# Three quarters of a down projection moved from one long matmul stage into the state loops of the following heads

## The chip, the cores and the metric

The kernel runs on one core of one Trainium2 chip. Its time is the device time of one launch, in microseconds (us); lower is better. The core has a matrix engine (TensorE, PE in the profile; its weight loads are PEld), a vector engine (VectorE, DVE), a scalar engine (ScalarE, ACT), GpSimd (POOL), and SyncE (SP), which here issues nearly all transfers. Sixteen DMA engines move data between memory and the on-chip buffer. Matmul results land in eight accumulation banks of 128 x 512 floats (`psum`).

## The reference

Two decoder layers run over 320 tokens at once: a prompt of 256 and eight sample sequences of 8. The change concerns layer 1, an mLSTM block with four heads; per head a sequence carries a state matrix C of 1024 x 1024 floats.

```
xm, z = split(xn @ w_up)                        # 4096 inner columns = 4 heads x 1024
q, k, v = blockdiag projections of conv(xm), xm
per head and sample sequence:
    num  = wprev * (q @ C) + (scores @ v);  h = num / max(|den|, exp(-m))
    C    = wC * C + (k * wS)^T @ v               # written out for every sequence
hn  = head_layernorm(h, norm_g)                 # per head
out = (hn + skip * xc) * silu(z)
y   = out @ w_down                              # 4096 x 2048
x   = x + y
```

After it come a mixture-of-experts layer (`moe`) and the last norm. All is float32.

## The kernel before

Activations lie transposed: 128 channels on the partitions, 320 tokens along the free side. `xm` holds the 32 chunks of inner channels (8 for each head), `m.x` the residual in 16 chunks of 128 output channels.

`mlstm` goes through heads 0 to 3. For each head there are three blocks of preparation (projections, scores, transposes), in which the layer norm of the head before it is also finished (`HeadNorm`, with `z` and the skip), and then a block with the **state loop**: eight sample sequences, and per sequence eight chunks c of 128 rows of C (512 KB each). For one chunk PE multiplies the queries with it (L2124), forms the outer product of keys and values in two halves (L2135, banks 5 and 6), and DVE scales the chunk and adds the halves (L2197). SP then stores the chunk (L2070) and loads a later one (L2065). The chunks live in eight slots; a slot is loaded again for the next sequence three chunks after its store was issued (`LAG`), and only once that store has landed. PE, DVE and SP each keep to the order written in the code and wait on semaphores. At chunks 1 and 2 PE also computes a piece of the prompt's new C (L2140), which ACT copies out (L2185) and SP stores in two halves at chunk 4 (L2081); at chunk 4 PE turns the keys and values of the next sequence (`turn`, L2114). The numerators of sequences 0 to 3 gather in bank 0 and those of 4 to 7 in bank 7; after the loop they are copied out by ACT and DVE (L2187, L2200).

After head 3's own layer norm, `linear` computes the whole of `out @ w_down`: 16 output tiles, each of 32 matmuls (L344) over all 32 inner chunks. With 32 chunks the eight weight slots of 1 MB make one column block of four tiles (`cbs` = 1), so there are four passes, and a pass can start only when DVE has added the four tiles of the one before (L398). One matmul in float32 is one matmul in the program and two instructions in the trace.

The lines at issue: `linear` L287 to L351 and L398; the state loop L2062 to L2207; the call L2237.

Of the kernel before, what the change touches and what calls it, by code (L numbers as in the profile page):

```python
# [13 lines left out]
ALU = mybir.AluOpType  # L14
# [6 lines left out]
P = 128  # L21
D = 2048
T_P = 256
B = 8
T_S = 8
T = T_P + B * T_S
# [6 lines left out]
H = 4  # L33
# [7 lines left out]
IC = DI // P  # L41
# [61 lines left out]
@contextmanager  # L103
def signal(m, name):

    yield m.signals.take()
    m.signals.held -= 1
# [170 lines left out]
def linear(nc, m, weights, kc, rhs, copy_to=None, conv=None, norm=None, fill=None):  # L278
# [6 lines left out]


    kg = kc // KPS  # L287
    cbs = NSLOT // kg
    width = TPB * P
    passes = weights.shape[1] // width // cbs  # L290
    w = weights.rearrange("(g k p) n -> p g k n", k=KPS, p=P)
# [1 line left out]
    with ExitStack() as ctx:  # L293
        def signals(name, n):
            return [ctx.enter_context(signal(m, f"{name}{i}")) for i in range(n)]

        landed = signals("landed", NSLOT)
        used = signals("used", NSLOT)
        tile_done = signals("tile_done", cbs)
        by_act = signals("by_act", cbs)  # L300
        by_dve = signals("by_dve", cbs)
# [4 lines left out]
        @block.sync  # L306
        def _(sp):
            def load(i, s):
                col = (i * cbs + s // kg) * width
                sp.dma_start(slots[:, s, :, :], w[:, s % kg, :, bass.ds(col, width)]).then_inc(landed[s], 16)  # L310

            for s in range(NSLOT):
                load(0, s)
            with sp.Fori(1, passes) as i:
                for s in range(NSLOT):
                    if s % kg < kg - 1:
                        sp.wait_ge(used[s], i)
                    else:
                        sp.wait_ge(tile_done[s // kg], i * TPB)
                    load(i, s)  # L320
            if fill is not None:
                for p in range(PAIRS):
                    sp.dma_start(fill[p * P:(p + 1) * P, :],
                                 m.x[:, :, :].rearrange("p c t -> p (c t)")[:, 0:D]).then_inc(filled, 16)
                sp.wait_ge(filled, 16 * PAIRS)

        @block.tensor
        def _(pe):
            if norm:
                norm.tensor(pe)  # L330
            with pe.Fori(0, passes) as i:
                for s in range(NSLOT):
                    cb, g = s // kg, s % kg
                    pe.wait_ge(landed[s], i * 16 + 16)
                    if g == 0:
                        if copy_to is not None:
                            pe.wait_ge(by_act[cb], i * TPB + TPB)
                        else:
                            pe.wait_ge(by_dve[cb], i * TPB + TPB)
                    for k in range(KPS):  # L340
                        if norm:
                            pe.wait_ge(norm.normed, g * KPS + k + 1)
                        for t in range(TPB):
                            mm = pe.matmul(m.psum[:, cb * TPB + t, 0:T], slots[:, s, k, t * P:(t + 1) * P],  # L344
                                           rhs(g * KPS + k), start=(g == 0 and k == 0),
                                           stop=(g == kg - 1 and k == KPS - 1))
                            if g == kg - 1 and k == KPS - 1:
                                mm.then_inc(tile_done[cb], 1)
                    if g < kg - 1:
                        mm.then_inc(used[s], 1)  # L350
# [1407 lines left out]
def mlstm(nc, m, I, O):  # L1758
# [35 lines left out]
    gates_and_z(nc, m, I, O, conv, xm, xc, wq, wk, wv, blk, bg, bgf, u_col, m0, wc_row, ml, wcol, n0)  # L1794

    c_slot = view(m.ring, 8192, HC, DH)
    s_t = [view(m.ring, 7424, T_P), view(m.ring, 7424 + T_P, P), view(m.ring, 7424 + T_P + P, 64)]
    vt = view(m.xn, 0, 3, DH)
    kt = view(m.xn, 3 * DH, 2, DH)
# [15 lines left out]
    for h in range(H):  # L1815
# [136 lines left out]

        states = ExitStack()
        landed = [states.enter_context(signal(m, f"state_landed{c}")) for c in range(HC)]
        c_in = I["state_mlstm_C"][0].rearrange("b h (c p) e -> b h c p e", p=P)
        LAG = 3
        with signal(m, "turned") as turned, signal(m, "copied") as copied, signal(m, "prompt_num") as prompt_num, \
                nc.Block() as block:
            @block.sync
            def _(sp):  # L1960
                for c in range(HC - LAG):
                    sp.dma_start(c_slot[:, c, :], c_in[0, h, c]).then_inc(landed[c], 16)

            @block.tensor
            def _(pe):
# [72 lines left out]
        with states as ctx:  # L2038
# [9 lines left out]
            num_kept = ctx.enter_context(signal(m, "num_kept"))  # L2048
            keys = ctx.enter_context(signal(m, "keys"))
            c_done = ctx.enter_context(signal(m, "c_done"))  # L2050
            c_kept = ctx.enter_context(signal(m, "c_kept"))
            c_stored = [ctx.enter_context(signal(m, f"c_stored{e}")) for e in range(2)]
            block = ctx.enter_context(nc.Block())
# [8 lines left out]
            @block.sync  # L2062
            def _(sp):
                def load(b, c):
                    sp.dma_start(c_slot[:, c, :], one(c_in, b)[h, c]).then_inc(landed[c], 16)  # L2065

                def sequence(b, more):
                    for c in range(HC):
                        sp.wait_ge(updated, b * (2 * HC) + (2 * c + 4))
                        sp.dma_start(one(c_out, b)[h, c], c_slot[:, c, :]).then_inc(stored[c], 16)  # L2070
                        if c < LAG:
                            if not (isinstance(b, int) and b == 0):
                                sp.wait_ge(stored[c - LAG + HC], b * 16)
                            load(b, c - LAG + HC)
                        elif more:
                            sp.wait_ge(stored[c - LAG], b * 16 + 16)
                            load(b + 1, c - LAG)
                        if c == HC // 2:
                            for e in range(2):
                                sp.wait_ge(c_kept, b * 2 + (e + 1))  # L2080
                                sp.dma_start(one(c_prompt, b)[:, e * 512:(e + 1) * 512],  # L2081
                                             c_stage[e]).then_inc(c_stored[e], 16)

                sequence(0, True)
                with sp.Fori(1, B - 1) as b:
                    sequence(b, True)
                sequence(B - 1, False)
                for c in range(HC):
                    sp.wait_ge(stored[c], 16 * B)
                for e in range(2):  # L2090
                    sp.wait_ge(c_stored[e], 16 + 16 * B)
# [18 lines left out]
            def _(pe):  # L2110
                def turn(i, odd):
                    for j, rep in enumerate((krep, vrep)):
# [3 lines left out]
                                           start=True, stop=True)  # L2116
                        mm.then_inc(turned, 1)

                def sequence(half, i, odd, last=False):
                    pe.wait_ge(queries, at(i, odd, 1, 1))  # L2120
                    for c in range(HC):
                        pe.wait_ge(landed[c], at(i, odd, 16, 16))
                        for j in range(4):
                            mm = pe.matmul(m.psum[32 * j:32 * j + 32, 7 * half, 0:256], q_one[odd][:, c, :],  # L2124
                                           c_slot[:, c, j * 256:(j + 1) * 256], start=False,
                                           stop=last and c == HC - 1, skip_group_check=True)
                        if c == HC - 1:
# [9 lines left out]
                        if c in (1, 2):  # L2137
                            pe.wait_ge(keys, at(i, odd, 1, 1))
                            for a in range(2):
                                mm = pe.matmul(m.psum[:, c, :], k_one[odd][:, a, :],  # L2140
                                               vt[:, a, (c - 1) * 512:c * 512], start=(a == 0), stop=(a == 1))
                            mm.then_inc(c_done, 1)
                        if c == HC // 2 and not last:
                            pe.wait_ge(c_kept, at(i, odd, 2, 2))
                            turn(i if odd == 0 else i + 1, 1 - odd)

                for half in range(2):
                    for j in range(4):
                        mm = pe.matmul(m.psum[32 * j:32 * j + 32, 7 * half, 0:256], s_t[2][0:64, 32 * half:32 * half + 32],
                                       vt[0:64, 2, j * 256:(j + 1) * 256], start=True, stop=False, skip_group_check=True)  # L2150
                mm.then_inc(read, 1)
                turn(0, 0)
                with pe.Fori(0, B // 4) as i:
# [3 lines left out]
                    sequence(1, i, 0)  # L2157
                    sequence(1, i, 1, last=i == B // 2 - 1)
                pe.drain().then_inc(num, 1)
                pe.wait_ge(num_kept, 2)  # L2160
                for half in range(2):
                    for r in range(2):
                        mm = pe.transpose(m.psum[:, 0, (2 * half + r) * P:(2 * half + r + 1) * P],
# [4 lines left out]
            def _(act):  # L2168
# [15 lines left out]
                            act.wait_ge(c_stored[e], at(i, odd, 16, 16))  # L2184
                            act.copy(c_stage[e], m.psum[:, 1 + e, :]).then_inc(c_kept, 1)  # L2185
                act.wait_ge(num, 1)
                act.copy(num_tok[:, 0, :], m.psum[:, 0, 0:256]).then_inc(num_kept, 1)  # L2187

            @block.vector
            def _(dve):  # L2190
                dve.sem_inc(updated, 2)
                with dve.Fori(0, B) as b:
                    for c in range(HC):
                        for e in range(2):
# [1 line left out]
                            part_c = c_slot[:, c, e * 512:(e + 1) * 512]  # L2196
                            dve.scalar_tensor_tensor(part_c, part_c, wcol[:, h, bass.ds(b, 1)], m.psum[:, 5 + e, :],  # L2197
                                                     ALU.mult, ALU.add).then_inc(updated, 1)
                dve.wait_ge(num, 1)
                dve.tensor_copy(num_tok[:, 1, :], m.psum[:, 7, 0:256]).then_inc(num_kept, 1)  # L2200
                dve.wait_ge(num, 2)
                turned_num = m.psum[:, 0, :].rearrange("p (g r j t) -> p g r j t", g=2, r=2, j=4)
                for half in range(2):
# [30 lines left out]
        (0, H * HC, O["p_m_n"].rearrange("a b h (c p) -> (a b h c) p", p=P)),  # L2234
        (H * HC, 9 * H * HC, O["s_m_n"].rearrange("a b h (c p) -> (a b h c) p", p=P))])

    linear(nc, m, I["l1_w_down"][0], IC, lambda k: xm[:, k, :])  # L2237


def build(nc, I, O):  # L2240
# [41 lines left out]
```

## Time and profile before

| | us |
|---|---|
| Median of 3 runs (lowest, highest) | 3639.81 (3634.59, 3644.52) |
| The profiled execution's own time | 3640.31 |
| its span in the trace | 3638.6 |
| PE busy over the span | 3081.8 (85%) |
| DVE busy | 990.0 (27%) |
| First matmul of the w_down stage to its last add | 2908.6 to 3190.8 |

Four state loops stand in the trace between 1908 and 2866 us, each about 171 us long; the w_down stage follows the last. A busy PE is one that has a matmul in flight, at either of its two clock levels (1.2 and 2.4 GHz); the granted clock (PEclk) tells which, as a share of the higher.

### The profile page before, as it was taken

To read this page: it belongs to the slowest core of one execution; us is meant where nothing else is said; L and a number is where in the kernel's file an instruction comes from. 1 tells how busy PE (TensorE), PEld (TensorE's weight loads), DVE (VectorE), ACT (ScalarE), POOL (GpSimd) and SP (SyncE) were. 2 spreads that over 40 slices of the span, in tenths; PEclk is the share of its full clock that TensorE was granted. 3 is DMA by queue.
4 is the path that set the end of the run, shared out by engine and by line. 5 is a ranking of instruction groups with operands and counts; after the bars stand their busy time and mean duration, and the time that the engine had idled before them with its cause. 6 is when DMAs were issued, how large, how long until landed. Compare 5 with 4: busy or idle time off the path is not lost. (4 is left out here: it accounts for less than half of the span.)

```text
span 3638.6 us, 36701 instructions
## 1 busy us (share of the span) xinstructions
PE 3081.8 (85%) x13501; PEld 1744.6 (48%) x13501; DVE 990.0 (27%) x2057; ACT 486.8 (13%) x845; POOL 90.8 (2%) x198
## 2 busy tenths in 40 slices
PE   7999669696999599999978778777778599969995
PEld 4777346473333377666753252242342266633333
DVE  1100232202111323210035555565465400021113
ACT  2000310002111201000111121121111100021112
POOL 0000000000000000000000000000000000000000
PEclk9999855798999799999988778778778699979997
DMA  4335010518899633153409919829739653188994
GB/s 160 127 117 220 29 47 0 190 46 311 343 357 385 227 119 123 40 168 119 142 37 378 393 52 406 342 98 418 284 148 418 261 176 122 46 311 344 352 390 159
DMA packets 277381, 764.64 MB, mean 210 GB/s; under 512 B 45744, under 2 KB 64780, under 8 KB 265716
## 3 DMA queue, kind: packets, MB, share of 16 engines
q1 hardware_dynamic: 266348, 709.51, 52.2%
q0 software_dynamic: 6688, 48.24, 3.5%
q10 hardware_dynamic: 4224, 5.24, 0.4%
q8 instruction: 80, 1.31, 0.1%
q14 instruction: 41, 0.34, 0.0%
HBM read 673.04 MB, written 215.70 MB: 244 GB/s over the span
## 5 line engine op out<-in xcount | busy, mean ns | idle before, releaser
L344 PE MATMUL psum<-x_norm,ring 128*128 128x320 f32 x2304 | 624.0, 434 | 8.0 <-DVE x_norm L274 8.0
L344 PEld LDWEIGHTS psum<-x_norm,ring 128*128 128x128 f32 x2304 | 439.6, 191 | 192.4 <-issue 10.9
L2197 DVE SCALAR_TENSOR_TENSOR ring<-ring,small,psum 128x512 f32<-128x512 f32 x512 | 357.0, 744 | 340.8 <-PE psum L2135 340.1
L344 PE MATMUL psum<-arena,ring 128*128 128x320 f32 x1536 | 420.1, 437 | 33.1 <-DMA ring<-in_l_w_out 22.6
L344 PEld LDWEIGHTS psum<-arena,ring 128*128 128x128 f32 x1536 | 294.5, 192 | 158.6 <-issue 35.7
L2124 PE MATMUL psum<-ring,x_norm 128*32 128x256 f32 x2048 | 194.2, 457 | 112.9 <-DMA ring<-in_state_mlstm_C 112.6
L1571 PE MATMUL psum<-x_norm,ring 128*128 128x320 f32 x1024 | 278.6, 434 | 6.8 <-DMA ring<-in_l_w_up 6.8
L1571 PEld LDWEIGHTS psum<-x_norm,ring 128*128 128x128 f32 x1024 | 195.1, 191 | 88.9 <-DMA ring<-in_l_w_up 7.3
L2135 PE MATMUL psum<-ring 72*128 72x512 bf16 x512 | 192.0, 448 | 14.3 <-DVE ring L2197 9.3
L671 PE MATMUL psum<-ring,x_norm 128*64 128x512 f32 x896 | 196.7, 594 | 0.0
L2124 PEld LDWEIGHTS psum<-ring,x_norm 128*32 128x32 f32 x2048 | 44.0, 117 | 262.7 <-DMA ring<-in_state_mlstm_C 173.9
L671 PE MATMUL psum<-arena,x_norm 128*64 128x512 f32 x768 | 168.5, 594 | 0.0
L398 DVE TENSOR_TENSOR x_resid<-x_resid,psum 128x320 f32 x32 | 15.6, 488 | 422.8 <-PE psum L344 421.7
L671 PEld LDWEIGHTS psum<-ring,x_norm 128*64 128x64 f32 x896 | 63.0, 137 | 123.0 <-issue 122.4
L2135 PEld LDWEIGHTS psum<-ring 72*128 72x128 bf16 x512 | 34.8, 100 | 163.8 <-issue 88.9
L924 DVE TENSOR_TENSOR arena<-arena,psum 128x256 f32<-128x256 f32 x26 | 10.9, 420 | 355.1 <-ACT arena L791 355.1
L698 PE MATMUL psum<-arena 128*64 128x512 f32 x448 | 101.6, 607 | 5.4 <-DMA arena<-in_moe_w_down 5.4
L257 ACT ACTIVATE arena<-x_resid 128x320 f32<-128x320 f32 x80 | 37.0, 468 | 504.4 <-PEq L293 290.6
L671 PEld LDWEIGHTS psum<-arena,x_norm 128*64 128x64 f32 x768 | 54.1, 137 | 104.8 <-issue 104.8
L698 PE MATMUL psum<-ring,arena 128*64 128x512 f32 x384 | 84.5, 592 | 4.4 <-DMA ring<-in_moe_w_down 4.4
L361 ACT COPY arena<-psum 128x320 f32 (+1 forms) x72 | 29.8, 428 | 432.6 <-PE psum L344 427.8
L454 DVE TENSOR_SCALAR arena<-arena,params (+1 forms) x40 | 16.7, 417 | 257.3 <-ACT arena L361 232.1
(392 smaller groups left out, 2678.1 us busy)
## 6 DMA issues: line engine op xcount, KB each, us to landing
ring<-in_state_mlstm_C SPq DMA_DIRECT2D x256, 512.0 KB, 8.7
out_s_m_C<-ring SPq DMA_DIRECT2D x256, 512.0 KB, 9.1
ring<-in_l_w_up SPq DMA_DIRECT2D x64, 1024.0 KB, 5.3
ring<-in_moe_w_gate SPq DMA_DIRECT2D x112, 512.0 KB
ring<-in_moe_w_up SPq DMA_DIRECT2D x112, 512.0 KB
arena<-in_moe_w_down SPq DMA_DIRECT2D x112, 512.0 KB
arena<-in_moe_w_gate SPq DMA_DIRECT2D x96, 512.0 KB
arena<-in_moe_w_up SPq DMA_DIRECT2D x96, 512.0 KB
```

Of the source, the lines that this page charges most:

```text
L257: act.activation(self.sq[:, c % 2, :], self.m.x[:, c, :], ACT.Square).then_inc(self.squared, 1)
L344: mm = pe.matmul(m.psum[:, cb * TPB + t, 0:T], slots[:, s, k, t * P:(t + 1) * P], rhs(g * KPS + k), start=(g == 0 and k == 0), stop=(g == ...
L361: act.copy(copy_to((i * cbs + cb) * TPB + t), m.psum[:, cb * TPB + t, 0:T]).then_inc(by_act[cb], 1)
L398: dve.tensor_tensor(x, x, ps, ALU.add).then_inc(by_dve[cb], 1)
L454: dve.tensor_scalar(y[:, 0:T_P], x[:, 0:T_P], w, self.m.prm[:, bass.ds(c + self.b, 1)], ALU.mult, ALU.add)
L671: mm = pe.matmul(m.psum[64 * i:64 * i + 64, 0, :], x_t[:, 4 * s + c, 64 * i:64 * i + 64], w[:, :, c, :], start=(s == 0 and c == 0), stop=( ...
L698: mm = pe.matmul(m.psum[64 * i:64 * i + 64, 4 + n, :], hid_t[:, k, 64 * i:64 * i + 64], w[:, n * 512:(n + 1) * 512], start=(k == 0), stop= ...
L924: dve.tensor_tensor(hid, act_g, m.psum[:, 0, FE:2 * FE], ALU.mult).then_inc(hid_done, 1)
L1571: mm = pe.matmul(m.psum[:, t, 0:T], slots[:, s, k, t * P:(t + 1) * P], m.XN[:, KPS * s + k, :], start=(s == 0 and k == 0), stop=(s == SLOT ...
L2124: mm = pe.matmul(m.psum[32 * j:32 * j + 32, 7 * half, 0:256], q_one[odd][:, c, :], c_slot[:, c, j * 256:(j + 1) * 256], start=False, stop= ...
L2135: pe.matmul(m.psum[:, 5 + e, :], k72[odd][0:ROWS72, c, :], v72[odd][0:ROWS72, 4 * e:4 * e + 4, :], start=True, stop=True).then_inc(outer, 1)
L2197: dve.scalar_tensor_tensor(part_c, part_c, wcol[:, h, bass.ds(b, 1)], m.psum[:, 5 + e, :], ALU.mult, ALU.add).then_inc(updated, 1)
```

## The change

The part of w_down that belongs to head h-1 (1024 of the 4096 rows) is multiplied inside the state loop of head h, for h = 1, 2, 3. Each of the eight sequences does two output tiles: PE runs eight matmuls for one tile after chunk 1 and eight for the other after chunk 5 (`project_down`), into bank 7, and DVE adds the tile to the residual after chunks 2 and 6. SP loads the weights of a sequence (128 x 8 x 256 floats, 1 MB) one sequence ahead, into two buffers in turn (`arena` where head 0's convolved inputs were, and `spare`). The numerators of both halves now share bank 0, so that bank 7 is free, and ACT alone copies them out. SP's loop over the sequences is unrolled. `linear` at the end handles only the 8 chunks of head 3, with two column blocks of four tiles in four slots, in two passes.

```diff
@@ linear
-    cbs = NSLOT // kg
+    cbs = min(NSLOT // kg, 2)
+    used_slots = cbs * kg
...
-                for s in range(NSLOT):
+                for s in range(used_slots):
@@ mlstm
+    down = [view(m.arena, IC * T, HC, 256), view(m.spare, 0, HC, 256)]
...
+        w_down = I["l1_w_down"][0][(h - 1) * DH:h * DH, :].rearrange("(k p) n -> p k n", p=P) if h else None
+
+        def load_down(sp, u):
+            sp.dma_start(down[u % 2], w_down[:, :, u * 256:(u + 1) * 256]).then_inc(down_landed[u % 2], 16)
...
                 for c in range(HC - LAG):
                     sp.dma_start(c_slot[:, c, :], c_in[0, h, c]).then_inc(landed[c], 16)
+                if h:
+                    load_down(sp, 0)
...
+                        if h and more and c == 0:
+                            if b:
+                                sp.wait_ge(down_done, 2 * b)
+                            load_down(sp, b + 1)
...
-                sequence(0, True)
-                with sp.Fori(1, B - 1) as b:
-                    sequence(b, True)
-                sequence(B - 1, False)
+                for b in range(B):
+                    sequence(b, b < B - 1)
...
+                def project_down(i, odd, r):
+                    pe.wait_ge(down_landed[odd], at(i, 0, 8, 16))
+                    pe.wait_ge(down_added, at(i, odd, 2, r + 1))
+                    for k in range(HC):
+                        mm = pe.matmul(m.psum[:, 7, 0:T], down[odd][:, k, r * P:(r + 1) * P], xm[:, (h - 1) * HC + k, :],
+                                       start=(k == 0), stop=(k == HC - 1))
+                    mm.then_inc(down_done, 1)
...
-                            mm = pe.matmul(m.psum[32 * j:32 * j + 32, 7 * half, 0:256], q_one[odd][:, c, :],
+                            mm = pe.matmul(m.psum[32 * j:32 * j + 32, 0, 256 * half:256 * half + 256], q_one[odd][:, c, :],
...
+                        if h and c in (1, 5):
+                            project_down(i, odd, c // 4)
...
-                act.copy(num_tok[:, 0, :], m.psum[:, 0, 0:256]).then_inc(num_kept, 1)
+                act.copy(num_tok.rearrange("p a e -> p (a e)"), m.psum[:, 0, :]).then_inc(num_kept, 1)
...
+                        if h and c in (2, 6):
+                            dve.wait_ge(down_done, b * 2 + (c // 4 + 1))
+                            x = m.x[:, bass.ds(b * 2 + c // 4, 1), :].squeeze(1)
+                            dve.tensor_tensor(x, x, m.psum[:, 7, 0:T], ALU.add).then_inc(down_added, 1)
-                dve.wait_ge(num, 1)
-                dve.tensor_copy(num_tok[:, 1, :], m.psum[:, 7, 0:256]).then_inc(num_kept, 1)
...
-    linear(nc, m, I["l1_w_down"][0], IC, lambda k: xm[:, k, :])
+    linear(nc, m, I["l1_w_down"][0][(H - 1) * DH:, :], HC, lambda k: xm[:, (H - 1) * HC + k, :])
```

PE, one sequence of head 1's state loop, from chunk 1 to the first matmuls of chunk 3, before (L2124 queries, L2135 outer product, L2140 the prompt's C):

```order
L2124 MATMUL psum<-ring,x_norm 32x256 x4
L2134 REGISTER_ALU
L2135 MATMUL psum<-ring 128x512
L2134 REGISTER_ALU
L2135 MATMUL psum<-ring 128x512
L2140 MATMUL psum<-x_norm,ring 128x512 x2
L2124 MATMUL psum<-ring,x_norm 32x256 x4
```

The same place of the change, where L2146, L2157 and L2162 are the same three steps and L2137 is the new one:

```order
L2146 MATMUL psum<-ring,x_norm 32x256 x4
L2156 REGISTER_ALU
L2157 MATMUL psum<-ring 128x512
L2156 REGISTER_ALU
L2157 MATMUL psum<-ring 128x512
L2162 MATMUL psum<-x_norm,ring 128x512 x2
L2134 ISA
L2135 ISA
L2137 MATMUL psum<-arena 128x320 x8
L2146 MATMUL psum<-ring,x_norm 32x256 x4
```

Eight float32 matmuls of 320 columns, and two waits ahead of them (L2134, L2135), stand between chunk 1 and chunk 2 on PE; eight more stand between chunks 5 and 6.

SP, the beginning of head 1's state loop in the change: the five chunks loaded ahead (L1970), then store (L2082), load (L2077) and the new weight load (L1961):

```order
L1970 DMA ring<-in_state_mlstm_C 128x1024 x5
L1961 DMA arena<-in_l_w_down 128x8x256
L1966 UNCONDITIONAL_BRANCH
L2074 UNCONDITIONAL_BRANCH
L2082 DMA out_s_m_C<-ring 128x1024
L2077 DMA ring<-in_state_mlstm_C 128x1024
L1961 DMA spare<-in_l_w_down 128x8x256
L2082 DMA out_s_m_C<-ring 128x1024
L2077 DMA ring<-in_state_mlstm_C 128x1024
```

Both L1961 rows are new; the rest stands in the order of before. The first weight load is issued ahead of the loop, the others one to a sequence behind chunk 0's store and load.

## Rows read from the trace of the kernel before

**Rows 1.** The page: span, granted clock and DMA share in 40 slices.

```profile
span 3638.6 us, 36701 instructions
PEclk9999855798999799999988778778778699979997
DMA  4335010518899633153409919829739653188994
```

**Rows 2.** Windows: head 3's loop, then a single sequence of it.

```profile
core 0: us, PE busy (x) PEld busy (x) DVE busy (x) ACT busy (x) POOL busy (x), PEclk, DMA share, GB/s
2695.00:2864.00 169.00, 138.54 (x821) 45.12 (x818) 87.84 (x126) 27.17 (x40) 3.99 (x6) 0.81 0.99 398
...
2800.40:2822.00 21.60, 18.16 (x104) 5.52 (x105) 10.68 (x16) 3.40 (x5) 0.67 (x1) 0.74 1.03 418
```

**Rows 3.** Timeline of PE through one sequence: start, us, work [idle before it].

```profile
2800.40 1.08 PE L2124 MATMUL psum<-ring,x_norm 128*32 128x256 f32 x8 [1.02 <-DMA ring<-in_state_mlstm_C]
...
2803.82 1.04 PE L2135 MATMUL psum<-ring 72*128 72x512 bf16 x2
2804.65 3.62 PE L2140 MATMUL psum<-x_norm,arena 128*128 128x512 f32 x4
2808.20 0.78 PE L2124 MATMUL psum<-ring,x_norm 128*32 128x256 f32 x8
2808.92 0.60 PE L2135 MATMUL psum<-ring 72*128 72x512 bf16 x2
2809.36 1.88 PE L2140 MATMUL psum<-x_norm,arena 128*128 128x512 f32 x4
2811.17 0.64 PE L2124 MATMUL psum<-ring,x_norm 128*32 128x256 f32 x8
...
2812.28 0.64 PE L2124 MATMUL psum<-ring,x_norm 128*32 128x256 f32 x8
...
2814.85 0.64 PE L2124 MATMUL psum<-ring,x_norm 128*32 128x256 f32 x8
...
2816.86 0.64 PE L2124 MATMUL psum<-ring,x_norm 128*32 128x256 f32 x8 [0.83 <-DMA ring<-in_state_mlstm_C]
...
2819.42 1.08 PE L2124 MATMUL psum<-ring,x_norm 128*32 128x256 f32 x8 [1.39 <-DMA ring<-in_state_mlstm_C]
...
2822.03 1.08 PE L2124 MATMUL psum<-ring,x_norm 128*32 128x256 f32 x8 [0.56 <-DMA ring<-in_state_mlstm_C]
```

**Rows 4.** Waits of PE, 2800.4 to 2843.6 us (two sequences): us, times, longest.

```profile
PE psum L2124 <- DMA ring<-in_state_mlstm_C: 7.0, 8, 1.4
```

**Rows 5.** Groups by line: the state update, and an add of a w_down tile.

```profile
L2197 DVE SCALAR_TENSOR_TENSOR ring<-ring,small,psum 128x512 f32<-128x512 f32 x512 | 357.0, 744 | 340.8 <-PE psum L2135 340.1
...
L398 DVE TENSOR_TENSOR x_resid<-x_resid,psum 128x320 f32 x32 | 15.6, 488 | 422.8 <-PE psum L344 421.7
```

**Rows 6.** Transfers: count, KB each, us from issue to landing.

```profile
ring<-in_state_mlstm_C SPq DMA_DIRECT2D x256, 512.0 KB, 8.7
out_s_m_C<-ring SPq DMA_DIRECT2D x256, 512.0 KB, 9.1
...
out_p_m_C<-ring SPq DMA_DIRECT2D x32, 256.0 KB, 8.7
out_p_m_C<-arena SPq DMA_DIRECT2D x32, 256.0 KB, 8.6
```

**Rows 7.** Timeline of the w_down stage: its first 50 matmul instructions, its last adds.

```profile
2908.62 16.55 PE L344 MATMUL psum<-arena,ring 128*128 128x320 f32 x50 [8.39 <-DMA ring<-in_l_w_down]
...
3188.74 2.10 DVE L398 TENSOR_TENSOR x_resid<-x_resid,psum 128x320 f32 x4 [67.76 <-PE psum L344]
```

**Rows 8.** Windows: 40 us inside w_down, and the start of the layer after it.

```profile
3000.00:3040.00 40.00, 40.00 (x150) 28.28 (x149) 0.00 (x0) 0.00 (x0) 0.00 (x0) 1.00 0.40 131
...
3200.00:3240.00 40.00, 22.97 (x109) 12.02 (x109) 19.06 (x72) 14.42 (x20) 5.74 (x6) 0.77 0.97 387
```

More of the change, by code:

```diff
@@ L295, in signals @@
             return [ctx.enter_context(signal(m, f"{name}{i}")) for i in range(n)]
-        landed = signals("landed", NSLOT)
-        used = signals("used", NSLOT)
+        landed = signals("landed", used_slots)
+        used = signals("used", used_slots)
         tile_done = signals("tile_done", cbs)
@@ L310, in load @@
                 sp.dma_start(slots[:, s, :, :], w[:, s % kg, :, bass.ds(col, width)]).then_inc(landed[s], 16)
-            for s in range(NSLOT):
+            for s in range(used_slots):
                 load(0, s)
             with sp.Fori(1, passes) as i:
-                for s in range(NSLOT):
+                for s in range(used_slots):
                     if s % kg < kg - 1:
@@ L331, in _ @@
             with pe.Fori(0, passes) as i:
-                for s in range(NSLOT):
+                for s in range(used_slots):
                     cb, g = s // kg, s % kg
@@ L1954, in mlstm @@
         landed = [states.enter_context(signal(m, f"state_landed{c}")) for c in range(HC)]
+        down_landed = [states.enter_context(signal(m, f"down_landed{i}")) for i in range(2)]
+        w_down = I["l1_w_down"][0][(h - 1) * DH:h * DH, :].rearrange("(k p) n -> p k n", p=P) if h else None
+        def load_down(sp, u):
+            sp.dma_start(down[u % 2], w_down[:, :, u * 256:(u + 1) * 256]).then_inc(down_landed[u % 2], 16)
         c_in = I["state_mlstm_C"][0].rearrange("b h (c p) e -> b h c p e", p=P)
@@ L2050, in mlstm @@
             c_done = ctx.enter_context(signal(m, "c_done"))
+            down_done = ctx.enter_context(signal(m, "down_done"))
+            down_added = ctx.enter_context(signal(m, "down_added"))
             c_kept = ctx.enter_context(signal(m, "c_kept"))
@@ L2148, in _ @@
                     for j in range(4):
-                        mm = pe.matmul(m.psum[32 * j:32 * j + 32, 7 * half, 0:256], s_t[2][0:64, 32 * half:32 * half + 32],
-                                       vt[0:64, 2, j * 256:(j + 1) * 256], start=True, stop=False, skip_group_check=True)
+                        mm = pe.matmul(m.psum[32 * j:32 * j + 32, 0, 256 * half:256 * half + 256],
+                                       s_t[2][0:64, 32 * half:32 * half + 32], vt[0:64, 2, j * 256:(j + 1) * 256],
+                                       start=(half == 0), stop=False, skip_group_check=True)
                 mm.then_inc(read, 1)
@@ L2159, in _ @@
                 pe.drain().then_inc(num, 1)
-                pe.wait_ge(num_kept, 2)
+                pe.wait_ge(num_kept, 1)
                 for half in range(2):
@@ L2191, in _ @@
                 dve.sem_inc(updated, 2)
+                dve.sem_inc(down_added, 1)
                 with dve.Fori(0, B) as b:
```

## The prediction

> **What bounds the kernel now.** I read the page's 40 slices first, then windows and timelines of the two stages that the change touches. In the slices the four state loops show up between the 22nd and the 31st as DMA shares of 7 to 9 with PEclk of 7 and 8; the w_down stage, the 33rd to the 35th, shows PEclk 9 with DMA shares of 5, 3 and 1 [rows 1]. So the two stages have opposite limits, and the windows say it in numbers. In a state loop the transfers run at 418 GB/s with a share of 1.03 within a sequence, that is all the time, and TensorE's granted clock is a mixture of its two levels, 0.74 in that sequence and 0.81 over the loop [rows 2]. In w_down PE has a matmul in flight in all of 40.00 us, at the higher level (2.4 GHz, share 1.00), and the transfers are busy 0.40 of the time [rows 8].
>
> One sequence of the loop, from one chunk 0 to the next, takes 2822.03 - 2800.40 = 21.6 us [rows 3]; the eight of a loop take about 171 us, so 21.5 is used. The timeline shows where PE stands still: ahead of chunks 6, 7 and 0 it waits 0.83, 1.39 and 0.56 us for a chunk to land [rows 3], 7.0 us over two sequences [rows 4]. A chunk's L2124 takes 0.64 us up to chunk 6 and 1.08 from chunk 7 on: the clock has fallen to its lower level (1.2 GHz) after those waits, and it is back only at the end of chunk 1's L2140 (3.62 us there, 1.88 at chunk 2) [rows 3]. None of this idling and slowness costs anything today, because the transfers end last.
>
> **The change part by part.** The sum is made against the profiled execution's 3640.3 us (span 3638.6 [rows 1], and 1.7 around it). The median of the runs is 3639.8, so no correction is needed.
>
> *What leaves the end.* The stage runs from 2908.62 to 3188.74 + 2.10 = 3190.84 us [rows 7]: 282.2 us. Of these, 512 matmuls are 1024 instructions at 40.00/150 = 0.267 us [rows 8], which is 273.1. The first 50 took 16.55 us and not 13.3 [rows 7], 3.2 us of a cold start at the lower level. The last add trails by about 0.6. What is left, 5.3, falls on the three changes of pass, in which PE waits for DVE's adds. The new stage has 128 matmuls, 68.3 us, the same cold start and tail, and its two passes use banks in turn, so the changes of pass cost nothing: 72.1 us. Its 8 MB of weights need some 21 us at the loop's rate, so they lie beside it. **Saved: 210.1 us.** The start of the stage, first load to first matmul, is as before.
>
> *What the loops take on: transfers.* A sequence moves 8 chunks in, 8 out, and two pieces of 256 KB out [rows 6], 8.5 MB (of 1024 KB); the weights make it 9.5. At the same rate the 21.5 us become 24.0. The weights are read in runs of 256 floats, the state in runs of 1024. The expert weights are read in runs of 256 floats too, and a window that is nearly filled with them gives 387 GB/s at a share of 0.97, 399 at one of 1.00, where the loop gives 418/1.03 = 406 [rows 2, 8]. That is 2% on one part in nine and is left out. The first of a loop's eight weight loads lies in the block ahead, where the DMA is nearly idle.
>
> *What the loops take on: matmuls.* Two tiles of eight matmuls are 32 instructions, 8.5 us at 0.267 [rows 8]. They sit in PE's own order, so what counts is how long PE needs for a sequence when nothing makes it wait for a transfer. At the higher level: chunk 2 with its L2140 takes 2811.17 - 2808.20 = 2.97, chunk 1 the same; chunk 3 takes 1.11; chunk 4 with its turn 2.57 [rows 3]. For chunks 5, 6, 7 and 0 I take DVE's pace, two updates of 0.744 = 1.49 [rows 5], since PE's own 0.64 + 0.60 is shorter. Together 2.97 + 2.97 + 1.11 + 2.57 + 4 x 1.49 = 15.6, and with the new matmuls **24.1 us**, as good as equal to the transfers' 24.0. The bounds follow. If the matmuls hide wholly behind the transfers, a sequence grows by 2.5 us. If they and the transfers are served one after the other, it grows by 8.5 + 2.5 = 11.0.
>
> I take +3.6, a period of 25.1: the longer of the two near-equal chains and 1.0 for their getting in each other's way. It lies near the lower bound because the queue of transfers is deep. A load lands 8.7 and a store 9.1 us after issue [rows 6], of which most is queueing behind other slots, and the gap that the new block opens is about as long: after chunk 1's update come L2140 (1.9), the tile (4.3) and chunk 2's matmuls (1.2), in which DVE gets no work and SP no store to issue, 7.4 us in all. The nearest gap in today's rows is the one from chunk 1's outer product to chunk 2's, 2808.92 - 2803.82 = 5.1 us [rows 3], and the DMA share stays at 1.03 through it [rows 2].
>
> What waits behind what: SP's weight load waits for the tiles of the sequence before, which PE has passed long before chunk 0's update lets SP get there. PE's two new waits are for weights issued a whole sequence earlier and for an add made four chunks earlier. DVE's adds are two of 0.488 us a sequence [rows 5] on an engine that is busy 11 of 21.6 us [rows 2], each for a tile finished one chunk before. I cost these three at nothing; without their cover an add is 1 us a sequence, 24 us in all, inside the range. Unrolling SP's loop, and moving the numerators' copy wholly to ACT, change the end of a loop by less than 1 us, in either direction.
>
> *The sum.* 24 sequences x 3.6 = 86 us. 3640.3 - 210.1 + 86 = **3516 us**.
>
> **A rule on the clock.** Today's rows show the lower level wherever short bursts alternate with waits for chunks, and the higher one after some dense microseconds of L2140 [rows 3]. The Trainium skill, "TensorE: Matmul & The Clock Gate", section "HAM oscillation — how this bites in real kernels", says the same in general: waits for transfers between short bursts make the array fall back to the slower clock, and matmul work in one piece keeps it warm. By that rule the new dense blocks after chunks 1 and 5 hold the higher level, and the rule and the sum agree on 24.1 us of PE. Read the other way, if the waits at chunks 6 to 0 remain, it gives the first rival below.
>
> **The rivals.**
>
> *The clock stays mixed.* PE is busy 18.2 us in a sequence at a mixed clock [rows 2]; the new matmuls at a mean of 0.81 take 8.5/0.81 = 10.5. With 18.2 and nothing else that is 28.7 us, +7.2, 173 us for 24: 3603. For it: the clock falls in each sequence now. Against it: what makes it fall are the waits for chunks, and a PE with 24.1 of 25 us to do has hardly any left. Chance 0.12 (3562 to 3640).
>
> *Only the transfers cost.* +2.5 a sequence, 60 us: 3490. For it: PE's chunks also shrink at the higher clock, so PE may keep up with some room. Against it: two chains of equal length seldom meet without loss. Chance 0.13 (3470 to 3497).
>
> *Slower: the blocks empty the queue.* While PE does a tile, DVE has nothing to update, SP nothing to store, and no slot comes free; if the transfers run dry for the 4.3 us of each tile, matmuls and transfers add up. +11.0 a sequence is 264 us: 3694. It decides in this direction from 210.1/24 = 8.75 us a sequence, that is from a dry time of (8.75 - 2.5)/2 = 3.1 us per tile. For it: the gap of 7.4 us is nearly the 8.7 to 9.1 from issue to landing, and eight slots are all there are. Against it: the 1 MB weight load adds 2.5 us to the queue ahead of chunk 1's block. Chance 0.05.
>
> That the change would not do what it says I leave out: the orders of PE and SP show the matmuls and loads where it puts them.
>
> **How the numbers follow.** The forecast holds 0.70, with growth of 2.4 to 5.5 us a sequence, 3497 to 3562. Eight in ten need a part of the neighbours: from 3485, which takes in most of the case that only transfers cost, to 3580, a good part of the way to the mixed clock. About 0.3% (11 us) is what a measurement of this kernel can tell from no change. Slower by more than that is the third rival, 0.05; between 3629 and 3651 there is the tail of the mixed clock, 0.02; faster has 0.93.
>
> **What would show it.** In the profile after: 256 instructions of L345 in a last stage of about 72 us; 768 of L2137 at 0.27 us each; a sequence of 25 us with a DMA share still near 1; a granted clock in heads 1 to 3 of 0.9 and more, while head 0's loop keeps 0.8 and its length. The forecast is wrong if L2137 takes 0.53 us an instruction (the lower level), or if the DMA share of these loops falls under 0.85 (the queue ran dry).

## The result, and the profile after

| | us |
|---|---|
| Before, median of the 4 runs beside it (lowest, highest) | 3642.1 (3634.6, 3644.5) |
| After, median of 4 runs (lowest, highest) | 3511.7 (3504.8, 3513.5) |
| Ratio, 95% interval | 0.9642 (0.9622 to 0.9662) |
| After, profiled execution; its span | 3512.0; 3510.3 |
| Forecast (range) | 3516 (3485 to 3580) |

The change is 130 us faster. The windows of the profile after, in the columns of [rows 2]: head 0's loop, the whole loops of heads 1 and 3, and two single sequences of head 3.

```profile
1910.00:2085.00 175.00, 144.77 (x848) 48.77 (x848) 89.15 (x130) 27.91 (x41) 5.89 (x9) 0.79 0.96 386
...
2171.70:2373.30 201.60, 190.90 (x1105) 92.70 (x1105) 93.94 (x144) 28.11 (x41) 5.87 (x9) 0.98 0.97 373
2748.20:2949.60 201.40, 190.91 (x1104) 92.78 (x1104) 93.87 (x144) 28.10 (x41) 5.88 (x9) 0.98 0.97 374
...
2804.50:2829.20 24.70, 23.70 (x136) 11.74 (x136) 11.56 (x19) 3.49 (x5) 0.67 (x1) 1.00 1.03 403
2878.00:2901.80 23.80, 22.63 (x137) 10.88 (x136) 11.76 (x19) 3.39 (x5) 0.67 (x1) 1.00 1.03 412
```

Head 0's loop, which got no tiles, still runs at a mixed clock (0.79). In the loops of heads 1 and 3 the granted clock is 0.98, where it was 0.81 in head 3 [rows 2]; PE has something in flight in 95% of the time, and the transfers are still at 1.03 in a sequence. Behind the first sequence of a loop (19.1 us) there are two kinds, some 24.9 us in the first half of a loop and 23.85 in the second.

The waits of PE over head 3's loop (2749 to 2948 us), as in [rows 4]:

```profile
PE psum L2157 <- DVE ring L2223: 6.7, 28, 0.3
PE psum L2157 <- ACT ring L2205: 0.7, 1, 0.7
PE psum L2146 <- issue: 0.2, 1, 0.2
```

No row for a chunk: the 7.0 us in two sequences that PE waited for them [rows 4] are gone. What PE still waits for is nearly all DVE, which must have taken an outer product out of its bank, 6.7 us in the loop or some 0.8 a sequence. By these rows PE's own order sets the pace; the experiments try it. One sequence on PE, as in [rows 3], from the turn (L2128) of chunk 4 on; L2137 are the new tiles:

```profile
2794.03 2.11 PE L2128 MATMUL psum<-identb,ring 128*72 128x128 bf16 x16
2796.07 0.64 PE L2146 MATMUL psum<-ring,x_norm 128*32 128x256 f32 x8
...
2797.08 4.47 PE L2137 MATMUL psum<-arena,spare 128*128 128x320 f32 x16
2801.49 0.64 PE L2146 MATMUL psum<-ring,x_norm 128*32 128x256 f32 x8
...
2807.32 1.88 PE L2162 MATMUL psum<-x_norm,ring 128*128 128x512 f32 x4
2809.04 4.47 PE L2137 MATMUL psum<-arena 128*128 128x320 f32 x16
...
2818.95 2.14 PE L2128 MATMUL psum<-identb,ring 128*72 128x128 bf16 x16
```

A tile follows the work before it without a gap and takes 4.47 us; L2146 is at 0.64 all the way, the higher level, also in chunks 7 and 0. In the sequences of the second half, which stand written out in the program, the turn takes 1.06 us instead of 2.1.

The last stage, as in [rows 7]:

```profile
2992.35 70.55 PE L345 MATMUL psum<-arena,ring 128*128 128x320 f32 x256 [8.50 <-DMA ring<-in_l_w_down]
...
3027.02 2.08 DVE L399 TENSOR_TENSOR x_resid<-x_resid,psum 128x320 f32 x4 [15.15 <-PE psum L345]
3044.24 2.08 DVE L399 TENSOR_TENSOR x_resid<-x_resid,psum 128x320 f32 x4 [15.14 <-PE psum L345]
3061.46 2.09 DVE L399 TENSOR_TENSOR x_resid<-x_resid,psum 128x320 f32 x4 [15.14 <-PE psum L345]
```

From 2992.35 to 3063.55 it is 71.2 us, where it was 282.2 [rows 7]: 211.0 saved. Taken from the first matmul of a state loop to its closing transposes, heads 1 to 3 took 175.9, 173.7 and 174.3 us before and take 201.6, 201.6 and 201.4 now: 80.7 added, 3.4 a sequence. Head 0's took 174.2 and takes 174.3. The balance is 130.3 us; the spans differ by 128.3.

### The profile page after: what moved, and what is told of

It is laid out like the page before. It is cut to its first block and busy times, and to the rows that moved or that the text cites. A ratio compares the mean times of both kernels' runs of the same rounds, so it can differ in the third digit from the quotient of the medians.

```text
span 3510.3 us, 35738 instructions
## 1 busy us (share of the span) xinstructions
PE 3024.9 (86%) x13501; PEld 1735.4 (49%) x13501; DVE 1003.8 (29%) x2101; ACT 487.5 (14%) x845; POOL 90.8 (3%) x198
## 5 line engine op out<-in xcount | busy, mean ns | idle before, releaser
L345 PE MATMUL psum<-arena,ring 128*128 128x320 f32 x768 | 211.0, 438 | 31.4 <-DMA ring<-in_l_w_out 22.9
L2157 PE MATMUL psum<-ring 72*128 72x512 bf16 x512 | 182.0, 404 | 33.0 <-DVE ring L2223 23.6
L2146 PE MATMUL psum<-ring,x_norm 128*32 128x256 f32 x2048 | 172.6, 410 | 25.6 <-DMA ring<-in_state_mlstm_C 24.8
L345 PEld LDWEIGHTS psum<-arena,ring 128*128 128x128 f32 x768 | 147.9, 193 | 94.4 <-issue 34.9
L2157 PEld LDWEIGHTS psum<-ring 72*128 72x128 bf16 x512 | 38.3, 97 | 184.1 <-DVE ring L2223 112.3
L2146 PEld LDWEIGHTS psum<-ring,x_norm 128*32 128x32 f32 x2048 | 41.4, 110 | 136.6 <-issue 90.0
L2137 PE MATMUL psum<-arena 128*128 128x320 f32 x384 | 107.7, 433 | 0.0
L2137 PE MATMUL psum<-arena,spare 128*128 128x320 f32 x384 | 107.3, 432 | 0.0
L2137 PEld LDWEIGHTS psum<-arena 128*128 128x128 f32 x384 | 73.6, 192 | 35.9 <-issue 7.6
```

Of the source, the lines that this page charges most:

```text
L2137: mm = pe.matmul(m.psum[:, 7, 0:T], down[odd][:, k, r * P:(r + 1) * P], xm[:, (h - 1) * HC + k, :], start=(k == 0), stop=(k == HC - 1))
L2146: mm = pe.matmul(m.psum[32 * j:32 * j + 32, 0, 256 * half:256 * half + 256], q_one[odd][:, c, :], c_slot[:, c, j * 256:(j + 1) * 256], sta ...
L2157: pe.matmul(m.psum[:, 5 + e, :], k72[odd][0:ROWS72, c, :], v72[odd][0:ROWS72, 4 * e:4 * e + 4, :], start=True, stop=True).then_inc(outer, 1)
```

## The experiments

Two chips were used, one for the first four kernels below (before: 3638.0 us, median of 13 runs) and one for the last four (before: 3639.9, 9 runs). Ratios and their intervals are the record's, to the kernel before on the same chip; they are not exactly the quotients of the medians. Where kernels ran on different chips, the ratios compare them better than the microseconds do.

**The rearrangement alone.**

```diff
-                if h:
-                    load_down(sp, 0)
...
-                        if h and more and c == 0:
-                            if b:
-                                sp.wait_ge(down_done, 2 * b)
-                            load_down(sp, b + 1)
...
-                        if h and c in (1, 5):
-                            project_down(i, odd, c // 4)
...
-                        if h and c in (2, 6):
+                        if False:
...
-    linear(nc, m, I["l1_w_down"][0][(H - 1) * DH:, :], HC, lambda k: xm[:, (H - 1) * HC + k, :])
+    linear(nc, m, I["l1_w_down"][0], IC, lambda k: xm[:, k, :])
```

> The change without its core: numerators in bank 0, SP's loop unrolled, ACT's single copy, but no weight loads and no tiles in the loops, and the whole of w_down in one stage at the end. Theory (the gain is the moved matmuls alone): within 5 us of the kernel before, 3636 to 3646, sequences of 21.5 us bound by transfers. Rival (the rearrangement itself makes the loops faster or slower): more than 10 us off, since four loops of eight sequences would show even 0.4 us each as 13.

Measured: 3639.5 us, ratio 1.0003 (0.9993 to 1.0013). The shared bank, the unrolled SP loop and ACT's single copy are worth nothing in either direction, within some 5 us. All of the gain comes with the tiles.

**Fewer weight loads.**

```diff
-                        if h and more and c == 0:
-                            if b:
-                                sp.wait_ge(down_done, 2 * b)
-                            load_down(sp, b + 1)
+                        if h and b == 0 and c == 0:
+                            load_down(sp, b + 1)
...
-                    pe.wait_ge(down_landed[odd], at(i, 0, 8, 16))
+                    pe.wait_ge(down_landed[odd], 16)
```

> The change with only the first two of the eight weight loads of each head; all later tiles multiply by those two buffers again (so y is built from wrong weights). It takes 18 MB out of the loops' transfers and leaves PE's work as it is. Theory (PE's own chain bounds the loops of heads 1 to 3): no gain, 3506 to 3514, sequences still 24.9 and 23.9 us. Rival (the transfers bound them, at 24.0 us a sequence): 18 loads less at 2.5 us, up to 45 us faster, 3467 or so.

Measured: 3509.3 us, ratio 0.9654 (0.9637 to 0.9672); the change's is 0.9642 (0.9622 to 0.9662). No gain. One sequence of each half, in the windows:

```profile
2766.97:2791.80 24.83, 23.75 (x137) 11.73 (x137) 11.79 (x19) 3.48 (x5) 0.67 (x1) 1.00 0.98 356
2866.55:2890.41 23.86, 22.69 (x138) 10.92 (x137) 11.82 (x19) 3.39 (x5) 0.67 (x1) 1.00 1.00 375
```

The transfers carry 356 and 375 GB/s instead of 403 and 412, and the sequences are as long as in the change. So the transfers do not bound these loops, and the 18 MB of weights removed here cost nothing. The DMA share hardly shows it: it is 0.98 and 1.00 with a tenth of a sequence's bytes gone. A share near 1 alone does not say that transfers are the limit; the GB/s and PE's waits for chunks have to be read with it.

**Two matmuls instead of eight.**

```diff
-                    for k in range(HC):
+                    for k in range(2):
                         mm = pe.matmul(m.psum[:, 7, 0:T], down[odd][:, k, r * P:(r + 1) * P], xm[:, (h - 1) * HC + k, :],
-                                       start=(k == 0), stop=(k == HC - 1))
+                                       start=(k == 0), stop=(k == 1))
```

> The change with 2 of the 8 matmuls in each of the 48 tiles of the loops; all weight loads stay. It leaves out 288 matmuls (6.4 us a sequence, 154 us in all). Theory (two chains of nearly equal length, PE's 24 to 25 us and the transfers' 24.0): the transfers take over at once, sequences of 23.7 to 24.0 us, 3495 to 3506, and the granted clock of these loops falls back to 0.8. Rival (matmuls and transfers add up): 100 to 154 us faster.

Measured: 3488.1 us, ratio 0.9591 (0.9575 to 0.9607), some 20 us faster than the change, and not 154. A sequence of head 3:

```profile
2793.40:2817.50 24.10, 19.73 (x113) 7.74 (x112) 11.96 (x19) 3.49 (x5) 0.67 (x1) 0.86 1.03 413
```

24.1 us at a share of 1.03, and the clock is mixed again, 0.86 here. PE waits for chunks, in head 3's loop:

```profile
PE psum L2146 <- DMA ring<-in_state_mlstm_C: 27.3, 27, 2.7
```

So the transfers set the length. The time lies below the 3495 to 3506 that I expected, and the gain is not where I looked for it: it comes from the first two sequences of a loop, which live on chunks loaded ahead (in head 3, from the turn ahead of the loop on, 15.9 and 19.2 us from turn to turn, 19.2 and 24.9 in the change). The five behind them take 23.9 to 25.9 us in the three loops, 24.5 on average, and 24.5 is their average in the change too. There the two chains are of one length. Three quarters of the new matmuls are worth 20 us where they would take 154 by themselves: the rest is hidden beside the transfers.

**Both tiles in one block.**

```diff
-                        if h and c in (1, 5):
-                            project_down(i, odd, c // 4)
+                        if h and c == 1:
+                            project_down(i, odd, 0)
+                            project_down(i, odd, 1)
...
-                        if h and c in (2, 6):
-                            dve.wait_ge(down_done, b * 2 + (c // 4 + 1))
-                            x = m.x[:, bass.ds(b * 2 + c // 4, 1), :].squeeze(1)
+                        if h and c in (1, 2):
+                            dve.wait_ge(down_done, b * 2 + c)
+                            x = m.x[:, bass.ds(b * 2 + (c - 1), 1), :].squeeze(1)
```

> The change with both tiles of a sequence after chunk 1, DVE adding the first after chunk 1 and the second after chunk 2. PE's work is the same; the stretch in which DVE has nothing to update and SP nothing to store grows from about 7 to 12 us. Theory (PE's chain bounds, the queue of transfers covers the gap, chunks land ahead): the second tile waits 0.5 to 1 us for the first add, and chunks 5 to 0 lose the rest that DVE had in the block after chunk 5: 0.5 to 2 us a sequence, 3520 to 3560. Rival (such a block empties the queue, and its dry time is lost): a dry time of 3 us or more a sequence, over 72 us slower than the change, 3585 or more, with a DMA share under 0.9 in the loops.

Measured: 3603.1 us, ratio 0.9914 (0.9897 to 0.9930), 91 us above the change's 3511.7. In the traces the three loops are 83.8 us longer than the change's, 3.5 a sequence. My expectation fell; the rival's came in. The windows of heads 1 and 3, then the waits in head 3:

```profile
2173.00:2406.70 233.70, 208.27 (x1104) 97.78 (x1104) 95.14 (x144) 28.13 (x41) 5.91 (x9) 0.90 0.86 319
2808.50:3037.00 228.50, 203.10 (x1104) 95.96 (x1104) 95.15 (x144) 28.02 (x41) 5.84 (x9) 0.92 0.88 326
```

```profile
PE psum L2146 <- DMA ring<-in_state_mlstm_C: 12.4, 11, 1.6
PE psum L2137 <- DVE x_resid L2229: 5.9, 8, 0.8
```

The DMA share falls from 0.97 to 0.86, and PE waits for chunks again, 1.6 us a sequence, besides 0.7 for the first tile's add. The clock takes most of the rest: it is 0.90 and 0.92 instead of 0.98, and PE is busy 203.1 us in head 3's loop instead of 190.9, 1.5 a sequence. SP's issues around a block show why the chunks come late. First the change, then this kernel (store L2082, load L2077, weights L1961; the second column is the time that issuing took):

```profile
2833.50 0.64 SPq L1961 DMA_DIRECT2D arena<-in_l_w_down  x1
2834.19 3.22 SPq L2082 DMA_DIRECT2D out_s_m_C<-ring  x1
2837.45 0.43 SPq L2077 DMA_DIRECT2D ring<-in_state_mlstm_C  x1
2840.73 0.34 SPq L2082 DMA_DIRECT2D out_s_m_C<-ring  x1
```

```profile
2874.35 0.48 SPq L1961 DMA_DIRECT2D spare<-in_l_w_down  x1
2874.88 3.93 SPq L2082 DMA_DIRECT2D out_s_m_C<-ring  x1
2878.85 0.81 SPq L2077 DMA_DIRECT2D ring<-in_state_mlstm_C  x1
2886.97 0.34 SPq L2082 DMA_DIRECT2D out_s_m_C<-ring  x1
```

In the change SP has nothing to issue for 2.9 us (2837.88 to 2840.73), here for 7.3 (2879.66 to 2886.97). The windows around the ends of these two stretches, the change's first:

```profile
2838.00:2841.00 3.00, 3.00 (x16) 1.03 (x14) 1.70 (x3) 0.00 (x0) 0.00 (x0) 1.00 1.05 384
```

```profile
2886.00:2888.00 2.00, 2.00 (x13) 0.59 (x12) 1.34 (x3) 0.53 (x2) 0.00 (x0) 1.00 0.27 111
```

The queue covers the first stretch and runs dry in the second. It does so in most sequences, not in all: in five of the first seven of this loop the share of some 2 us falls under 0.7.

**The change again**, beside the next three.

> The change itself, once more, beside the next kernels on one chip: 3511, within 0.2%.

Measured: 3508.0 us, ratio 0.9638 (0.9625 to 0.9651).

**PE's loop written out.**

```diff
-                with pe.Fori(0, B // 4) as i:
+                for i in range(B // 4):
                     sequence(0, i, 0)
```

> The change with PE's loop over sequences 0 to 3 written out, as sequences 4 to 7 are already, so that the register arithmetic between the 16 matmuls of a turn is gone (2.1 us a turn in the loop, 1.06 written out). Theory (PE's chain bounds heads 1 to 3): their sequences 0 to 3 go from 24.9 to 23.9 us, 12 x 1.0 = 12 us faster than the change, 3499; head 0's loop, which the transfers bound, stays. Rival (the transfers bound the loops of heads 1 to 3): no difference, 3508 to 3514.

Measured: 3499.0 us, ratio 0.9615 (0.9601 to 0.9628). All five runs (3496.2 to 3500.9) lie below all five of the change on the same chip (3504.7 to 3512.0); the medians differ by 9.0. A sequence of the first half of head 3's loop:

```profile
2807.30:2831.15 23.85, 22.68 (x138) 10.91 (x137) 11.82 (x19) 3.40 (x5) 0.67 (x1) 1.00 1.03 414
```

24.9 has become 23.85. The turn's 16 matmuls are the same in both; what stands between them in the looped half is register arithmetic, one row ahead of each weight load. The trace of the change has these rows (count; ns least, median, most), 16 for each looped turn, and that of this kernel has none:

```profile
L2128 PEldq FUSED_REGOPS  x256: 46/46/83, 1928.4 to 2845.6; - x128
```

Where the transfers end last it costs little: head 0's loop takes 173.1 us here and 174.4 in the second trace of the change. It began to count when PE ended last. Of the 12 us forecast 9 came in the medians, and why not 12 stays open: in the traces the loops of heads 1 to 3 are 14.9 us shorter (590.4 and 605.3), and stretches that the edit leaves alone are some 4 us longer, while the five runs of the change lie 7 us apart. Two later sequences take 24.1 and 24.3 us, as the transfers' do.

**Written out, and the tiles after chunks 0 and 6.** Besides the edit above:

```diff
-                        if h and c in (1, 5):
+                        if h and c in (0, 6):
                             project_down(i, odd, c // 4)
...
-                        if h and c in (2, 6):
+                        if h and c in (1, 7):
```

> As the kernel with PE's loop written out, and the tiles after chunks 0 and 6 instead of 1 and 5, so that PE has a tile to do where it now waits for DVE between outer products (chunks 6, 7, 0 and 1). Theory: PE's chain loses some 1 us a sequence, but the transfers' 24.0 us are already the length of a sequence there, so 0 to 8 us faster than with the loop alone written out, 3491 to 3499, and PE waits for chunks again. Rival (the transfers are not next, 23.9 is PE's length alone): the whole 1 us counts, 24 us faster, 3475.

Measured: 3497.5 us, ratio 0.9609 (0.9596 to 0.9622): not to be told from the one before, 1.5 us apart. The time is within what I expected, the reason was only half right. The first sequences are still 23.85 us, so moving the tiles took nothing off PE's chain. The later ones are longer, and in these PE waits for chunks (2827.05 to 2899.72 us, three sequences):

```profile
2803.20:2827.05 23.85, 22.76 (x137) 10.79 (x136) 11.78 (x19) 3.39 (x5) 0.67 (x1) 1.00 1.03 414
2827.05:2851.39 24.34, 22.58 (x137) 10.76 (x136) 11.87 (x19) 3.39 (x5) 0.67 (x1) 1.00 1.04 413
2851.39:2875.45 24.06, 22.58 (x137) 10.77 (x136) 11.87 (x19) 3.39 (x5) 0.67 (x1) 1.00 1.04 414
```

```profile
PE psum L2146 <- DMA ring<-in_state_mlstm_C: 2.6, 3, 1.0
```

The transfers are the limit there, at 413 and 414 GB/s. These two kernels are the fastest of those that do all of the work. In the first sequences of a loop PE sets the pace with 23.85 us, in the later ones the transfers with 24.1 to 24.8; neither chain can give much alone.

**One column block in the last stage.**

```diff
-    cbs = min(NSLOT // kg, 2)
+    cbs = 1 if kg == 2 else NSLOT // kg
```

> The change with the last stage in one column block of four tiles in two slots, so four passes that each wait for the adds of the one before, as in the kernel before. Theory (a change of pass costs 5.3/3 = 1.8 us): three of them, 5 us slower than the change, 3514 to 3518, the stage 77 us long instead of 72. Rival (the changes of pass are hidden): no difference.

Measured: 3512.8 us, ratio 0.9652 (0.9639 to 0.9666). The medians are 4.8 us apart, but the intervals of this and the change overlap: the times alone leave it open. The trace shows its passes:

```profile
3010.10 17.49 PE L345 MATMUL psum<-arena,ring 128*128 128x320 f32 x64 [0.69 <-DVE x_resid L399]
3028.28 17.49 PE L345 MATMUL psum<-arena,ring 128*128 128x320 f32 x64 [0.69 <-DVE x_resid L399]
3046.47 17.49 PE L345 MATMUL psum<-arena,ring 128*128 128x320 f32 x64 [0.69 <-DVE x_resid L399]
```

From pass to pass 18.18 us, against 17.22 between the adds of the change's stage: 0.96 for a change of pass, 2.9 for three. Half of my 1.8 each.

## Why the prediction was right, step by step

*The saving.* 210.1 forecast, 211.0 measured. Within it one term was mis-sized: the three changes of pass are worth 2.9 us and not 5.3. The other 2.4 lie in the matmul itself, 17.22/64 = 0.269 us an instruction and not the 0.267 read off a window cut into whole instructions.

*The loops.* 86 us forecast, 80.7 measured; 3.4 a sequence instead of 3.6. The period was put together from a chain of 24.1 and 1.0 for PE and the transfers getting in each other's way. The chain without any wait for a chunk is 23.85 us (second halves, and most of the first half with PE's loop written out), so 24.1 was close; in it the four chunks at DVE's pace were 6.0 where 5.5 was measured, and the two tiles 8.5 where it was 8.8.

The 1.0 was wrong in its cause, and that its size came out is in part luck. PE has no row of waiting for a chunk in these loops (in the second trace of the change, 1.2 us in head 1's). Two other things lengthen them, and both come from taking one sequence for all eight. One is the turn, 2.1 us in PE's loop and 1.06 in the sequence of the second half from which I read 2.57 for chunk 4: with a looped one read as well, the chain would have been 24.1 and some 25.1, against 23.85 and 24.9 measured. The other is the start of a loop. From turn to turn, the first two sequences of heads 1 to 3 took 14.3 and 19.3 us on average before, on chunks loaded ahead, and take 19.1 and 24.9 now, some 5 more each. The five behind them went from 21.6 to 24.5, by 2.9.

One bound was added up wrongly: with a growth of 2.4 us a sequence the time is 3488 us, and 3497 belongs to 2.8. The measured 3.4 lies above both.

*The transfers.* 24.0 us forecast for a sequence with its weights. Where they are the bound (two matmuls instead of eight), the sequences behind the first two of a loop take 23.9 to 25.9, 24.5 on average; before, these took 21.6, where I used 21.5. Whether the weights' short runs cost 2% on a ninth, 0.05 us, cannot be seen in such a spread.

*The clock.* 0.9 and more forecast, 0.98 measured, with 0.79 in head 0. When tiles shrink to a quarter and PE waits for chunks again, the clock in a sequence falls to 0.86. With both tiles in one block the dense work is longer, but PE waits for chunks too, and the loops are at 0.90 and 0.92. So in these runs the clock fell where PE waited 27.3 or 12.4 us a loop for chunks, and not where it waited 2.6 us in three sequences (1.00, tiles after chunks 0 and 6); denser blocks alone did not hold it. The rule of the Trainium skill ("TensorE: Matmul & The Clock Gate", section "HAM oscillation — how this bites in real kernels") is that waits for transfers between short bursts bring the slower clock, and dense work the faster; these traces agree. That PE does not wait for chunks is, by these runs, why the mixed-clock rival (3603) did not come.

*Only the transfers cost* (3490): not so, since PE ended last; the two kernels with PE's loop written out come within 9 us of it.

*Slower, the blocks empty the queue.* Not in the change, whose loops keep a share of 0.97. But the mechanism exists: with both tiles in one block it costs 3.5 us a sequence and eats 91 of 130 us, a part of it by way of the clock and of the wait for the first add. I set the gap from one chunk's outer product to the next (7.4 us forecast and measured in the change, 13.5 in the block of both tiles shown above) against the 8.7 to 9.1 us from issue to landing [rows 6], and that comparison pointed the right way in both cases. I had then expected the longer block to be covered too, at some 12 us, and it was not. Where between 7.4 and 13.5 us it begins was not tried.

*Costed at nothing.* The rearrangement is (1.0003). The weight loads' waits are too: PE has no row of waiting for them. DVE's adds were not taken out by themselves. PE is seen to wait for an add only in the two-tile block; in the change it waits some 0.8 us a sequence for DVE's updates, and what part of that the adds ahead of them cause is not shown.

## What to carry to other kernels

When one stage is bound by transfers and another by PE, work moved between them is worth what the slower of the two new chains leaves; add up PE's chain without any transfer wait and at the higher clock, for each kind of sequence that the code has, looped and written out. Once PE becomes the bound, instructions that were free (register arithmetic between matmuls) count, and are worth taking out. Read the first sequences of a loop by themselves, since they live on what was loaded ahead. Split the moved work into pieces that the queue of transfers outlasts: the same matmuls in one block cost 91 us here.

## What the runs showed of the hardware that was not expected

Sixteen small matmuls took 2.1 us with register arithmetic between them and 1.06 without, at the same granted clock (1.00). The arithmetic itself is 16 x 46 ns = 0.74 us of the difference. So what stands between them, and not the matmuls, set their time.

Behind a 1 MB weight load in runs of 256 floats, SP was slow to issue the next 512 KB store: 0.34 us behind the first such load of each loop, and 0.93 to 4.71 behind the other 21. Over the whole kernel, the longest issue of such a store is 4.7 us in the change, 1.6 with the weight loads cut to two a head, and 1.3 in the kernel before; the median is 0.33 in all three. So these loads hold up what SP issues behind them. Whether it is their short runs or their size that does it was not separated. Here it cost nothing: with the loads cut to two a head the sequences are as long, and the slow issue falls into a block in which SP had little else to issue.
